# The gate and up weights of a seven-product layer go round two places instead of three

## The reference, cut to what matters

```python
def swiglu(u, w_gate_up, w_down):
    gate, up = jnp.split(u @ w_gate_up, 2, axis=-1)
    return (jax.nn.silu(gate) * up) @ w_down

mod = c_act @ ada_w[layer] + ada_b[layer]     # second block, computed beside the gated layer
```

## Time and profile before

| | |
|---|---|
| median of 3 runs | 2929.49 us (2929.01 to 2931.03) |
| span of the profiled execution | 2929.7 us (its run 2931.55 us) |
| PE busy | 2814.9 us, 96% of the span |
| DVE, ACT, POOL busy | 1872.1, 1297.8, 723.1 us |
| gated layer's 88 units | some 929 to 1369 us |

### The profile page before, as it was taken

One profiled execution on the slowest core, in us unless ns is written; L12 is line 12 of the kernel. 1 busy time (PEld: TensorE's weight loads), 2 busy tenths in 40 slices (PEclk: granted clock), 3 DMA queues, 4 the chain that ended last, 5 costly groups with the idle time before them and its releaser, 6 DMA issues.

```text
span 2929.7 us, 37370 instructions
## 1 busy us (share of the span) xinstructions
PE 2814.9 (96%) x14198; PEld 2349.2 (80%) x14198; DVE 1872.1 (64%) x2550; ACT 1297.8 (44%) x2086; POOL 723.1 (25%) x925
## 2 busy tenths in 40 slices
PE   8999999999999999999999999999999899999998
PEld 6878787778887788887888678788888777888986
DVE  6564475764455788887334736789878745318974
ACT  5321347432444322222211435678767624427851
POOL 0000003300002566663000011456545300004520
PEclk9999999999999999999999999999999999999999
DMA  4111333232311344446311323100001231131032
GB/s 142 58 43 52 129 107 128 98 115 87 100 58 47 115 148 141 146 148 225 109 48 46 112 65 88 49 1 12 12 15 37 101 108 44 51 94 64 18 116 72
DMA packets 201521, 245.46 MB, mean 84 GB/s; under 512 B 11776, under 2 KB 152320, under 8 KB 199808
## 3 DMA queue, kind: packets, MB, share of 16 engines
q1 hardware_dynamic: 184320, 186.37, 20.0%
q0 software_dynamic: 9104, 28.32, 3.2%
q10 hardware_dynamic: 7920, 28.38, 2.9%
HBM read 192.11 MB, written 46.20 MB: 81 GB/s over the span
## 4 chain that ended last, share of the span: by engine, by line
PE 84%; DVE 7%; ACT 3%; POOL 2%; issue 2%; DMA 1%; SPq 0%; ACTq 0%; DVEq 0%; POOLq 0%
PE P L348 46%; PE P L289 5%; PE P L291 5%; PE P L290 5%; PE P L286 5%; PE P L2713 4%; PE P L317 2%; PE P L2727 2%; PE P L2726 1%; PE P L1111 1%; PE P L1585 1%; PE P L3319 1%; POOL T L2975 1%; POOL WS L3456 1%; DVE WST L3431 1%
## 5 line engine op out<-in xcount | busy, mean ns | idle before, releaser
L273 DVE TENSOR_TENSOR wl<-wf,wh 128x1024 fp32r<-128x1024 f32 (+3 forms) x163 | 192.7, 1182 | 665.5 <-ACT wh L265 665.0
L265 ACT ACTIVATE wh<-wf 128x1024 fp32r<-128x1024 f32 (+3 forms) x163 | 166.9, 1024 | 766.2 <-PE P L348 703.0
L348 PE MATMUL P<-XH,wh 128*128 128x512 f32 (+1 forms) x1232 | 385.0, 394 | 6.8 <-DVE TMP L1388 2.5
L348 PE MATMUL P<-XL,wh 128*128 128x512 f32 (+1 forms) x1232 | 381.7, 391 | 0.0
L348 PE MATMUL P<-XH,wl 128*128 128x512 f32 (+1 forms) x1232 | 380.6, 390 | 0.0
L2975 POOL TENSOR_TENSOR T<-T,WST 128x512 f32<-128x512 f32 x256 | 260.9, 1040 | 220.3 <-DVE WST L2945 197.5
L348 PEld LDWEIGHTS P<-XH,wh 128*128 128x128 f32 (+1 forms) x1232 | 229.0, 187 | 62.2 <-issue 12.7
L348 PEld LDWEIGHTS P<-XH,wl 128*128 128x128 f32 (+1 forms) x1232 | 230.2, 187 | 51.1
L348 PEld LDWEIGHTS P<-XL,wh 128*128 128x128 f32 (+1 forms) x1232 | 229.9, 187 | 51.2
L289 PE MATMUL P<-FO,U 128*128 128x512 f32 x616 | 242.5, 394 | 8.0 <-DVE U L1833 6.7
L290 PE MATMUL P<-FO,U 128*128 128x512 f32 x616 | 240.7, 391 | 0.0
(11 more groups left out here) (483 smaller groups left out, 6281.3 us busy)
## 6 DMA issues: line engine op xcount, KB each, us to landing
AW<-ada_t POOLq DMA_DIRECT2D x96, 256.0 KB, 3.4
wf<-gu_units SPq DMA_DIRECT2D x88, 256.0 KB, 3.0
H<-scratch_h SPq DMA_DIRECT2D x32, 512.0 KB, 6.5
wf<-w_in SPq DMA_DIRECT2D x28, 512.0 KB, 3.8
scratch_h<-H SPq DMA_DIRECT2D x24, 512.0 KB, 5.9
scratch_g<-T ACTq DMA_DIRECT2D x22, 512.0 KB, 3.0
scratch_f<-T ACTq DMA_DIRECT2D x22, 512.0 KB, 3.2
wf<-odd_w_in SPq DMA_DIRECT2D x20, 512.0 KB, 3.8
```

The source lines that it names most:

```text
L265: e.activation(self.sb["wh"][i % 2][:, 0:m], self.sb["wf"][i % 2][:, 0:m], ACT.Copy).then_inc(*self.s.w_hi.up(i))
L273: e.tensor_tensor(l, f, h.bitcast(F32), ALU.subtract).then_inc(*self.s.w_lo.up(i))
L348: ins = e.matmul(self.P[slot][0:m, t:t1], w, x[:, k, t:t1], start=first and k == 0, stop=last and k == kb - 1)
```

## The change

The third place goes. `unit(u)` chooses between two places, and `act_unit(u)` waits until TensorE is done with unit `u - 2` (units 0 and 1: with the tile of `wo` whose slab lay in that place). ScalarE and VectorE convert unit `u + 1` and no longer `u + 2` at the start of step `u`. On the way in unit 1 moves from `j == 6` to where unit 2 was in `j == 7`, and unit 2 into step 1. On the way out slab 0 of `w_down` is converted in step 87 and slab 1 behind blocks 3 to 6, since both lie where the last two units lie; blocks 0 to 2 stay in step 86. `pool_unit`, `sp_unit`, `pool_ada` and `ada_unit` are the same code as before.

```diff
--- before.py
+++ after.py
@@ -1747,7 +1747,6 @@
                     self.act_form(e, j // 2, 1)
             if j == 6:
                 self.act_unit(e, 0)
-                self.act_unit(e, 1)
                 e.wait_ge(*self.s.mm.to(("wo", "through", 3)))
                 self.act_scaled(e, 2, 0)
                 self.act_scaled(e, 2, 1)
@@ -1755,7 +1754,7 @@
                 e.wait_ge(*self.s.mm.to(("wo", 7)))
                 self.act_scaled(e, 3, 0)
                 self.act_scaled(e, 3, 1)
-                self.act_unit(e, 2)
+                self.act_unit(e, 1)
                 self.act_form(e, 3, 0)
                 self.act_form(e, 3, 1)
         self.act_tiles(e, "wo", empty)
@@ -1777,10 +1776,9 @@
                 self.dve_form(e, p, 1)
             if j == 6:
                 self.dve_unit(e, 0)
-                self.dve_unit(e, 1)
                 self.form_sums(e, self.s.dve, 2)
             if j == 7:
-                self.dve_unit(e, 2)
+                self.dve_unit(e, 1)
                 self.dve_form(e, 3, 0)
                 self.dve_form(e, 3, 1)
         self.dve_tiles(e, "wo", empty)
@@ -1793,7 +1791,7 @@
     def unit(self, u):
 
         at = (self.no["wo", 6] % 2, self.no["wo", 7] % 2)
-        i = (2, *at)[u % 3]
+        i = at[u % 2]
         return self.sb["UH"][i], self.sb["UL"][i]
 
     def unit_done(self, u):
@@ -1820,10 +1818,7 @@
     def act_unit(self, e, u):
         if u < UNITS:
             e.wait_ge(*self.s.pool.to(("s", u)))
-            if u > 2:
-                e.wait_ge(*self.s.mm.to(self.unit_done(u - 3)))
-            elif u:
-                e.wait_ge(*self.s.mm.to(("wo", 5 + u)))
+            e.wait_ge(*self.s.mm.to(self.unit_done(u - 2) if u > 1 else ("wo", 6 + u)))
             e.activation(self.unit(u)[0][:, :], self.raw(u)[:, 128:1024], ACT.Copy).then_inc(*self.s.w_hi.up(("u", u)))
 
     def dve_unit(self, e, u):
@@ -2024,7 +2019,7 @@
         for u in range(UNITS):
             m, k = u // 4, u % 4
             if u:
-                self.act_unit(e, u + 2)
+                self.act_unit(e, u + 1)
             if u == 2:
                 self.act_roots(e, "n3", self.bank_of(7)[:, 0:8], 0, D, s.mm.to(("n3", "roots")))
             if u == 3:
@@ -2035,13 +2030,11 @@
             if k == 2 and m:
                 store(m - 1)
             if u == UNITS - 2:
-                e.wait_ge(*s.mm.to(self.unit_done(UNITS - 3)))
-                self.act_weights(e, self.no[("dn", 0), 0])
                 for b in range(3):
                     self.act_ffn_block(e, b)
             if u == UNITS - 1:
                 e.wait_ge(*s.mm.to(self.unit_done(UNITS - 2)))
-                self.act_weights(e, self.no[("dn", 0), 1])
+                self.act_weights(e, self.no[("dn", 0), 0])
             if k == 3:
                 e.wait_ge(*s.mm.to(("gu", m, 0)))
                 if m:
@@ -2055,6 +2048,8 @@
                 e.activation(self.sb["AA"][:, :], self.sb["AA"][:, :], ACT.Silu).then_inc(*s.act.up("silu c"))
         for b in range(3, 7):
             self.act_ffn_block(e, b)
+        e.wait_ge(*s.mm.to(self.unit_done(UNITS - 1)))
+        self.act_weights(e, self.no[("dn", 0), 1])
         silu(PAIRS - 1)
         store(PAIRS - 1)
         self.act_tiles(e, ("dn", 0), lambda e, j: self.act_ffn_block(e, 7 + j))
@@ -2113,7 +2108,7 @@
         for u in range(UNITS):
             m, k = u // 4, u % 4
             if u:
-                self.dve_unit(e, u + 2)
+                self.dve_unit(e, u + 1)
             if u == 2:
                 v = self.dve_roots(e, "n3", 8, 0, D, self.bank_of(7)[:, 0:8])
                 self.dve_diagonal(e, "n3", v, T[2], 8)
@@ -2123,11 +2118,10 @@
             if k == 1 and m:
                 product(m - 1)
             if u == UNITS - 2:
-                self.dve_weights(e, self.no[("dn", 0), 0])
                 for b in range(3):
                     self.dve_ffn_block(e, b)
             if u == UNITS - 1:
-                self.dve_weights(e, self.no[("dn", 0), 1])
+                self.dve_weights(e, self.no[("dn", 0), 0])
             if k == 3:
                 first_drains(m)
             for h in range(96):
@@ -2136,6 +2130,7 @@
         last_drains(PAIRS - 1)
         for b in range(3, 7):
             self.dve_ffn_block(e, b)
+        self.dve_weights(e, self.no[("dn", 0), 1])
         normed(PAIRS - 1)
         product(PAIRS - 1)
 
@@ -3697,9 +3692,9 @@
                      [128, 7, 512], F32) for p in range(4)]
     sb["FAF"] = put("FAF", "A", 0, [128, 7, 2, S], F32)
     sb["FXF"] = put("FXF", "X", 0, [128, 8, 2, S], F32)
-    sb["UH"], sb["UL"] = ([put(f"U{i}{n}", *((("W", 8 * K), ("W", 17 * K), ("A", 56 * K))[n][0],
-                                             (("W", 8 * K), ("W", 17 * K), ("A", 56 * K))[n][1] + 3584 * i),
-                               [128, 896], F32R) for n in range(3)] for i in range(2))
+    sb["UH"], sb["UL"] = ([put(f"U{i}{n}", *((("W", 8 * K), ("W", 17 * K))[n][0],
+                                             (("W", 8 * K), ("W", 17 * K))[n][1] + 3584 * i),
+                               [128, 896], F32R) for n in range(2)] for i in range(2))
     sb["FA"] = put("FA", "A", 0, [128, 7, 2, S], F32R)
     sb["FX"] = put("FX", "X", 0, [128, 8, 2, S], F32R)
     sb["AW"] = [put(f"AW{i}", "X", 28 * K + 2 * K * i, [128, 512], F32)[:, :] for i in range(2)]
```

## The result

The changed kernel takes 2944.87 us (2936.99 to 2950.74) where the kernel before takes 2929.25 on the same chip: 1.0053 times as long, 95% interval 1.0038 to 1.0068. It is slower by 15.6 us; 8 were forecast, and the range held. The profiled execution of the changed kernel has a span of 2941.2 us (its run 2943.0), 11.5 us more than before.

What follows compares the result with a forecast made beforehand. From 967 to 1360 us TensorE, busy 391.71 of 393.00 us, bounds the kernel, so the change can only lose there by late weights. Way in -5, middle +9, way out +4 make +8: 2929.5 + 8 = 2937.5 us, range 2927 to 2946.

Steps and rivals of the forecast that it cites:

- The three places: Way in, middle and way out of the layer, forecast at -5, +9 and +4 us.
- Way in: Up to unit 4's start: unit 4 starts near 961.1, not 966.12; 5.0 us won, bounds 2.5 and 5.5.
- Middle: Units end to end, 967 to 1360 us: 9 us lost to late weights less drain stalls, bounds -2 and 25.
- 14 x 0.8 = 11 us: Middle: 14 units have two ada steps; each such place makes weights 0.8 us late, bounds 0 and 1.9.
- the forecast chain t + 15.1: Middle: conversion, load, sums of 3.3, ada load, ada step, conversion, plus 1.2 us late first conversion; due at t + 14.3.
- some 2 us of drain stalls: Middle: of TensorE's 3.0 us waiting for VectorE's PSUM drain, some 2 us were to go.
- The clock low beyond unit 1: Sign that the forecast is wrong: TensorE's clock low after unit 1.
- Way out: From unit 87 into w_down: blocks 0 to 2 shift by 3.5 to 4.3 us; 4 us lost, bounds 3 and 5.
- Two places suffice: Rival: sums stay near 1.8 us, no ada pair is late, middle -2 to +2; 2926.5 to 2930.5 us; chance 0.22.
- The whole loop saturates: Rival: middle loop 10.15 us exceeds two units' 9.52, every unit 0.3 us late; middle +22, 2950 us; chance 0.13.
- Faster: Rival: way in gives 5.5, drain stalls go, way out hidden by blocks landing sooner; -7.5, 2922 us; chance 0.05.

Runs made afterwards that it cites:

- e8_one_input: The changed kernel with VectorE's two norms and product replaced by one-operand reductions, norm factors and up part left out; 2936.48 us, ratio 1.0025.
- e1_three_places: The changed kernel, its order kept, with the third place and its wait put back; 2943.83 us, ratio 1.0051.
- e3_blocks_first: The changed kernel, but SP issues blocks 0 to 2 ahead of slab 1 of w_down; 2940.25 us, ratio 1.0047.
- e6_two_all: The changed kernel with four AW buffers, root first, unit 2's conversion ahead of form 3, blocks first and spread among slab 0 and first drains; 2923.43 us, ratio 0.9981.
- e2_four_ada: The changed kernel with four buffers AW instead of two, GpSimd loading pieces four ahead; 2925.72 us, ratio 0.9993.
- e5_no_pairs: The changed kernel without the last 14 of the 96 modulation pieces, so no step has two; 2923.71 us, ratio 0.9980.

## Why the prediction was right and wrong

**Direction and places: right.** The three places, their signs and the chain of the middle (conversion, load, sums, piece, conversion) were as told.

**Way in: right, 0.8 us short.** Counted from unit 0, unit 1 was to start at 10.9 and did so at 10.89; unit 2 at 20.9, measured 20.72; the table load at 22.7, measured 22.47; the diagonal ready at 26.5, measured 26.54. Unit 4 was to start at 31.7 and did at 32.59: the copy at L2027 ended 0.8 us later than forecast, since the conversion ahead of it waited until 954.88 for its sums. The gain was 4.2 and not 5.0.

**Middle: the mechanism right, the term mis-sized** (9 forecast, 22.3 measured), in three ways.

- *Late weights.* 14 x 0.8 = 11 us was forecast, and about 10 came (9.5 in units with k = 2, 0.6 with k = 1), but not 14 times 0.8: three times 2.1, three times 0.7 to 1.3, little elsewhere. In the worst case the forecast chain t + 15.1 became t + 16.43 (t is 1080.33): the sums took 4.8 us where 3.3 was taken (the bound was 4.4), the piece landed in 4.0 and not 3.4; the first conversion and the load were 0.7 us quicker. e8_one_input shows why just the sums beside norms and product. Which pair costs weights depends on its step: the three of 2.1 us come one unit behind the pairs in steps 17, 29 and 41 (k = 1), the three of 0.7 to 1.3 two units behind those in steps 52, 64 and 76 (k = 0). Behind pairs in steps with k = 2 or 3 it is the drains that are late (units 8, 12, 24, 48, 60, 72 and 84). So 14 places of one size was the wrong count.
- *Drains.* The forecast let some 2 us of drain stalls go. They grew from 2.4 to 8.9 us in units with k = 0. I had costed the drains only in the list before, where the conversion ahead of them was long done; in the new list they stand behind a conversion and behind late pieces. This step had the wrong sign.
- *The clock.* The sum had no term for what a stall does after it ends. Three stalls of 2.1 us were each followed by a unit at the lower level, 1.7 us each, 5.2 in all. The clock low beyond unit 1 was named as a sign of being wrong, and here it is. This part is the least steady of the three: e1_three_places and e3_blocks_first have one such unit each.

Together 2 + 6.5 + 5.2 less 1 for the weights make 12.7 of the 13.3 us that were missing.

**Way out: the size right** (4 forecast, 4.7 measured), **the path in part**. Unit 87's low half ended 3.2 us behind the start of unit 86 (the upper end of 2.3 to 3.2), and ScalarE took block 2 at 13.5 us behind that start and not 9.5, 4.0 later, as forecast. But the last wait became slab 0's conversion, behind the blocks, which I had costed at nothing, and the matmuls of slab 0 behind it ran at the lower clock, for which the sum had no term: TensorE reached block 3 without a wait. e6_two_all, which moves the blocks' issue, slab 0's conversion and the first drain at once, has a way out of 11.7 us; no run parts the three. That 16.2 us came with the same order in e2_four_ada makes the closeness of 4 to 4.7 partly luck.

**The rest**: 11.4 us of the profiled execution's gain and loss lie outside the layer, 9.1 of them behind block 3 at a better clock. The forecast had nothing there. One execution of each kernel doesn't tell whether the medians hold the same share. That the range held is partly luck: by these two executions the layer lost 22.9 us, and 2929.25 + 22.9 = 2952 us would have been above it.

**The rivals.** *Two places suffice* fell for this kernel, and holds for the loop itself (e5_no_pairs, -0.03). *The whole loop saturates* named a middle of +22, close to what came, by a mechanism that e5_no_pairs excludes: the number alone would have picked the wrong cause. *Faster* fell: the blocks didn't land sooner (block 0 took 7.3 us from issue to landing, 5.2 before).

## What to carry to other kernels

Where engines execute lists in order, taking a buffer away moves everything that is queued behind its new wait, a different stream's loads too. Cost the queues, the loop and the wait apart: here the missing place itself cost nothing that the runs show, and the late pieces behind the sums most of what the middle lost. For every stall that a sum says will go away, ask what now stands ahead of the instruction that ended it.

## What the runs showed of the hardware

In the changed kernel TensorE stood idle within steady work for 1.92 to 1.94 us ahead of units 19, 31 and 43, and each time the lower clock level followed (matmuls of 0.63 us and not 0.40, unit 31 in 6.47 us); 1.13 us ahead of unit 67 were not followed by it. The length of the idle time alone doesn't settle it: in e1_three_places 1.94 us ahead of unit 43 were not followed by the lower level, 2.79 us ahead of unit 19 were. GpSimd's four sums take 1.8 us beside an idle VectorE (from 1091.90 us in the changed kernel) and 4.8 beside a gapless row of two-operand instructions, which themselves grow (a piece of 0.75 us takes 0.95, a conversion of 1.09 takes 1.31): both engines pay. Behind the layer, the same matmuls took 8 us less in one kernel's execution than in the other's, with the same idle time (60.9 and 61.5 us), so by the granted clock, which is over half of what this change moved.
